# Expert matrices stored whole in their tile instead of interleaved by rows of 256 columns

## What is computed

```python
h = jax.nn.silu(jnp.einsum('td,edf->tef', xt, w1)) * jnp.einsum('td,edf->tef', xt, w3)
h = h * gates[:, :, None].astype(h.dtype)
y = jnp.einsum('tef,efd->td', h, w2)
# exp_w1, exp_w3: (32, 1024, 256)   exp_w2: (32, 256, 1024)
```

## Time and profile before

| | us |
|---|---|
| median of 3 runs | 661.05 (660.33 to 662.53) |
| span of the profiled execution | 656.5 |
| median less that span | 4.55 |
| of the span: to the first `up` of the experts | about 341 |
| the experts, to the last `down` | about 281 |
| combination and last norm | about 34 |

### The profile page before, as it was taken

How to read it: one execution, slowest core, us unless ns; L and a number is a source line. 1 busy time by engine, 2 the same in 40 slices (tenths; PEclk the granted TensorE clock), 3 DMA queues, 4 the chain that set the end, 5 groups by cost and what they waited for, 6 DMA issues and landing times. The chain is left out here.

```text
span 656.5 us, 6560 instructions
## 1 busy us (share of the span) xinstructions
PE 510.5 (78%) x2320; PEld 296.6 (45%) x2320; DVE 230.2 (35%) x519; ACT 142.6 (22%) x267; POOL 79.2 (12%) x129
## 2 busy tenths in 40 slices
PE   3999999999999989999459839395684929478800
PEld 3788888358888733545333313132231313123200
DVE  3353112694987565233721111111020111101158
ACT  7211044704256352212100000000010000001123
POOL 4000000100211211000030111102011111101014
PEclk9899999999999979999559869788795969779955
DMA  9403110412341439210969999999999999969263
GB/s 300 151 0 129 57 72 12 152 53 77 100 165 64 144 122 308 116 44 22 342 230 331 375 376 337 388 336 394 336 369 376 355 379 331 398 198 381 82 280 130
DMA packets 90494, 144.62 MB, mean 220 GB/s; under 512 B 6489, under 2 KB 72197, under 8 KB 85856
## 3 DMA queue, kind: packets, MB, share of 16 engines
q1 hardware_dynamic: 79608, 100.57, 45.9%
q10 hardware_dynamic: 3888, 28.31, 10.6%
q0 software_dynamic: 6976, 15.44, 7.1%
HBM read 137.49 MB, written 15.10 MB: 232 GB/s over the span
## 5 line engine op out<-in xcount | busy, mean ns | idle before, releaser
L1390 PE MATMUL ps<-XNT,WC 128*128 128x260 f32 x640 | 144.8, 386 | 1.2 <-PE ps L1390 0.6
L1390 PEld LDWEIGHTS ps<-XNT,WC 128*128 128x128 f32 x640 | 121.9, 192 | 23.3 <-issue 4.0
L1629 PE MATMUL ps<-WC,XRC 128*64 128x512 f32 x128 | 69.0, 700 | 66.7 <-DMA GY<-in_exp_w 66.7
L1294 DVE TENSOR_TENSOR XRC<-ps,XRC 128x256 f32<-128x256 f32 x16 | 6.8, 424 | 184.2 <-ACT XRC L810 184.2
L1629 PE MATMUL ps<-GY,XRC 128*64 128x512 f32 x128 | 69.0, 701 | 0.0
L1629 PEld LDWEIGHTS ps<-WC,XRC 128*64 128x64 f32 x128 | 19.8, 162 | 107.7 <-issue 107.6
L1629 PE MATMUL ps<-SLOT,XRC 128*64 128x512 f32 x240 | 59.0, 617 | 2.4 <-DMA SLOT<-in_exp_w 2.4
L1551 PE MATMUL ps<-WC,GY 128*128 128x512 f32 x128 | 58.6, 611 | 1.0 <-DVE GY L1184 0.6
L810 ACT ACTIVATE XRC<-ps 128x256 f32<-128x256 f32 x16 | 6.1, 383 | 209.2 <-PE ps L1629 209.2
L609 POOL DMA_INDIRECT expert_rows<-T,SIDX x16 | 16.1, 1008 | 236.9 <-ACT T L824 220.1
L1551 PEld LDWEIGHTS ps<-WC,GY 128*128 128x128 f32 x128 | 24.4, 196 | 29.4 <-issue 28.2
(11 more groups left out here) (273 smaller groups left out, 587.7 us busy)
## 6 DMA issues: line engine op xcount, KB each, us to landing
SLOT<-in_exp_w SPq DMA_DIRECT2D x32, 1024.0 KB, 12.4
WC<-in_exp_w SPq DMA_DIRECT2D x18, 1024.0 KB, 13.3
GY<-in_exp_w SPq DMA_DIRECT2D x16, 1024.0 KB, 17.7
WC<-in_exp_w ACTq DMA_DIRECT2D x14, 1024.0 KB, 8.5
SLOT<-in_exp_w ACTq DMA_DIRECT2D x13, 1024.0 KB, 8.8
WC<-in_w_in SPq DMA_DIRECT2D x6, 2048.0 KB, 9.2
WC<-in_w_out SPq DMA_DIRECT2D x2, 2048.0 KB, 7.8
X<-in_x_prompt SPq DMA_DIRECT2D x4, 512.0 KB, 4.7
```

Source lines behind the costliest of these rows:

```text
L1294: dve.tensor_tensor(HG[p], PS[2 + p][:, FE:2 * FE], HS[p], ALU.mult).then_inc(s_hg, 1)
L1390: ins = pe.matmul(ps[:, 0:HALF], WC[:, j % 2, k, m * P:(m + 1) * P], XNT[:, k, hf * HALF:(hf + 1) * HALF], start=(k == 0), stop=(k == KD - 1))
L1629: ins = pe.matmul(PS[2 + p][at:at + CAP, :], XGT[p][:, k, at:at + CAP], weights[two][0][:, k, :], start=(k == 0), stop=(k == KD - 1), tile ...
```

## The change

w1 of an expert lies whole in the first 2048 columns of the slot and w3 whole in the second 2048. The DMA of either writes 2048 consecutive numbers per partition, and a step of `up` reads 256 numbers at 256k and 256 at 2048 + 256k.

```diff
-        W13 = [s[:, 0:4096].rearrange("p (k f) -> p k f", k=KD) for s in (SLOT0, SLOT1, WCF, GYF)]
+        W13 = [s[:, 0:4096].rearrange("p (w k f) -> p w k f", w=2, k=KD) for s in (SLOT0, SLOT1, WCF, GYF)]
...
-        W13_KEPT = XNF[:, 0:4096].rearrange("p (k f) -> p k f", k=KD)
+        W13_KEPT = XNF[:, 0:4096].rearrange("p (w k f) -> p w k f", w=2, k=KD)
...
                 for half, w in enumerate((exp_w1, exp_w3)):
-                    sp.dma_start(w13[:, :, half * FE:(half + 1) * FE],
+                    sp.dma_start(w13[:, half],
                                  w[0, e].rearrange("(p k) f -> p k f", k=KD)).then_inc(s_w13[slot], 16)
...
-                        ins = pe.matmul(PS[2 + p][at:at + CAP, :], XGT[p][:, k, at:at + CAP], weights[two][0][:, k, :],
+                        ins = pe.matmul(PS[2 + p][at:at + CAP, :], XGT[p][:, k, at:at + CAP], weights[two][0][:, :, k, :],
                                         start=(k == 0), stop=(k == KD - 1), tile_position=(0, at), skip_group_check=True)
```

## The result

The changed kernel takes 629.41 us against 661.26 us (medians of 4 runs each), a ratio of 0.9515 with a 95% interval of 0.9488 to 0.9541: 31.9 us less, where 629 was forecast.

A forecast was written before the change was run, and what follows sets the result against it. The prediction took the full DMA engines to bound the expert turns; loads 25.8, order 3.0 and end 3.1 us sum to 31.9, leaving a 624.6 us span, plus 4.5 around it: 629 us, range 620 to 645.

The forecast's parts named there:

- The bound: Expert loop: moving the weights' bytes through the DMA engines sets the 37.64 us turn; TensorE works only 25.87 us of it.
- The loads: w13 loads in 8 KiB pieces at 420 instead of 348 GB/s: 50 loads save 0.516 us each, 25.8 us.
- The order: On the DMA engines, equal pieces let w13 and w2 share evenly, so GY lands earlier once: 3.0 us, bounds 0 to 5.0.
- a rival: Odd pair's `up`: only four SLOT loads are queued, engines run dry and half the gain is lost: 645 us, chance 0.08.
- The end: From 578.60 us to the last pair: four faster loads, less waiting and part of a slow `up` save 3.1 us (2.1 to 4.3).
- The sum: Experts' gains of 25.8 + 3.0 + 3.1 = 31.9 us leave a 624.6 us span; 4.5 us around it makes 629.
- TensorE's read: `up`'s moving operand as two runs of 256 numbers, 8 KiB apart, costs nothing; upper bound a doubled `up`, 7.09 us more.
- The rival's arithmetic: In `up`, the two-run read halves the rate and TensorE becomes the bound: 683 us, chance 0.05.
- What is late next: In the turns, w2 comes late but covered; gathers a few us later at worst, covered by a shortened wait for GY.
- Engines that run dry: Odd pair's `up`: SP issues nothing new, the DMA engines empty and half the gain is lost: 645 us, chance 0.08.
- Pieces that don't matter: w13 loads: 348 GB/s is what one queue alone gives, so piece size changes nothing: 661 us, chance 0.05.
- The estimate from the overhead per packet: w13 loads: about 3 cycles per packet make 8 KiB pieces 7.5% or 0.226 us a load cheaper, 11.3 us in all.

The follow-up runs named there:

- e8: The changed kernel unedited, run once more beside e9 on the same chip: 628.32 us, ratio 0.9496 to the kernel before.
- e1: Changed kernel with its new layout, but every w13 load in 1 KiB pieces again (two DMAs per matrix): 663.62 us against 660.44 for the kernel before, ratio 1.0051.
- e2: Changed kernel with w1 and w3 alternating in blocks of 512 numbers, so w13 pieces of 2 KiB: 645.28 us, ratio 0.9761 to the kernel before.
- e3: Changed kernel with w1 and w3 alternating in blocks of 1024 numbers, so w13 pieces of 4 KiB: 632.49 us, ratio 0.9551 to the kernel before.
- e6: Kernel before the change with the w2 loads in 1 KiB pieces too, like its w13 loads: 666.53 us, ratio 1.0090 to the kernel before.
- e4: Changed kernel with each gather issued one step earlier, ahead of the scatter it stood behind: 626.64 us, ratio 0.9499 to the kernel before.
- e9: Changed kernel with each gather issued one step earlier, timed again beside the changed kernel on the same chip: 627.49 us, ratio 0.9478 to the kernel before.
- e5: Changed kernel with the w2 loads in 1 KiB pieces (two DMAs per matrix on ACT's queue), w13 in 8 KiB: 645.05 us, ratio 0.9758 to the kernel before.

## Why the prediction was right

*The bound.* Right. The DMA engines' rate sets the turn before and after; 8 KiB pieces move it from 37.64 to 33.18 us (33.5 forecast), with TensorE's work in it unchanged.

*The loads.* Right, slightly too low. 420 GB/s were taken for a queue of 8 KiB pieces; without a pause the profile shows 427: 50 × (3.013 − 2.456) = 27.9 us instead of 25.8. In e8, the same kernel once more, the same stretch shows 424, which makes it 27.0. e1 shows that the pieces are the cause, e2 and e3 that their price falls with their number.

*The order.* Right in direction, priced too high. The first `up` behind a long wait of TensorE starts 42.2 us into the experts (385.88) instead of 49.2 (390.40), the five turns give 5 × 4.46 = 22.3 us, and the end, from there to the last `down`, takes 41.3 instead of 43.6 us. That is 7.0 + 22.3 + 2.4 = 31.7. Less 27.9 for the loads and 2.4 for the end, 1.4 us are left for the order, where 3.0 were taken. They lie before the first of these `up`, as forecast: ten of the 50 loads are moved there, 5.6 us, and the other forty in the turns, 22.3 us, which is all that the turns gave. So small a remainder is not clear of noise: in e8 a turn takes 33.49 instead of 33.18 us, 1.5 us in five. e6 shows that even sharing gives time without any faster load, 8 us there; in the changed kernel no run separates it from the loads.

The sum has no term for the pause at the end of each odd `up`, which stands in the prediction under a rival only. In the kernel before the engines were at 0.89 and 0.59 for two microseconds where 1.10 is full, about 0.65 us lost in this turn:

```profile
437.00:438.00 1.00, 1.00 (x6) 0.31 (x4) 0.01 (x1) 0.00 (x0) 0.00 (x0) 1.00 0.89 261
```

Over the five turns the lowest microsecond there has 0.56 to 0.64 before and 0.78 to 0.92 after, so the pause shrinks. What that is worth stays open: the sum leaves nothing for it, and no kernel removed it alone.

*The end.* 2.4 us instead of 3.1: the last pair's wait fell from 2.64 to 0.47 us.

*The sum.* That 629 was met to half a microsecond is in part luck. The loads gave about 2 us more than their term, the order and the end about 2 less; and the span came out at 628.2 instead of 624.6, with 1.8 us around it instead of 4.5.

*TensorE's read.* Costs nothing, as taken: 7.09 us per `up` in both, and e1. The rival's arithmetic also held: 683 forecast for a doubled `up`, 678.49 measured.

*What is late next.* This step failed. I had w2 and a shorter wait for GY of 5 to 8 us; in fact the wait for GY all but vanished and TensorE waits for the gathered rows, 46.3 us in all. The landing of the loop's 14 gathers (L597), least, median and longest, before and after:

```profile
DMA to landing us min/median/max: 7.6/8.2/9.2
```

```profile
DMA to landing us min/median/max: 7.6/13.2/14.6
```

"A few us later at worst" is 5.0 us at the median, but their cover was gone, since GY came earlier still. It cost nothing that e4 and e9 could show; the engines stay full either way, with a DMA share of 1.00 in e8 and 0.99 in e9 from 343 to 552 us.

*The rivals.* Engines that run dry would have shown a turn only 2 us shorter. Pieces that don't matter fall with e1 to e3. The Trainium skill ("DMA: Bandwidth & Descriptors", "Specifications") lists 512 bytes as the least transfer for line rate; in this kernel pieces of 1 KiB ran at 348 and of 8 KiB at 427 GB/s from one queue, so that being above 512 bytes was not enough. The estimate from the overhead per packet that the Trainium skill gives ("DMA: Bandwidth & Descriptors", "Why small descriptors are slow"), 7.5%, has the right sign and under half of the measured 18%.

## What to carry to other kernels

Where the DMA engines are full, look at the size of the pieces before the number of bytes: a destination that breaks a consecutive source into short runs is paid for on every load, while a matmul's moving operand could be broken into two runs for nothing. When several queues share the engines, they take turns by pieces, and the one with the larger pieces gets the more bytes, so give the load that is needed first pieces no smaller than its neighbours'. Small pieces also hold the engine that issues them, so look at what waits behind that engine. And a new name at the top of the waits is not a new bound: move it away and see whether the time follows.

## What the runs showed of the hardware

The rate of one queue by the size of its pieces was 348, 386, 411 and 427 GB/s at 1, 2, 4 and 8 KiB, about 0.08 us for each further piece of a load of 1 MiB over 128 partitions. Queues of equal pieces took turns packet by packet, 128 to 127 in 5 us, and so did queues of unequal ones, 209 to 211. In the turns shown, SP was busy for 19.69 us with issuing four loads in 1 KiB pieces and for 1.89 us with four in 8 KiB pieces; ACT was busy for 7.36 us with two w2 loads in 1 KiB pieces (e5) and for 0.85 us in 8 KiB pieces. A moving operand of two runs of 256 numbers, 8 KiB apart, cost nothing: 7.09 us for an `up` as with one run.
